# Expert outputs added into DRAM accumulators by accumulating scatters, in place of a slot store and a final gather

## What is computed

```python
def routed_experts(xt, idx, gate, w_exp_gu, w_exp_down):
    ...
    def run_block(args):
        tok, g, e = args
        return swiglu(x_pad[tok], w_exp_gu[e], w_exp_down[e]) * g[:, None]
    out = lax.map(run_block, (row_tok.reshape(n_blocks, MOE_BLOCK), ...))
    return jnp.zeros((T + 1, D), xt.dtype).at[row_tok].add(out.reshape(R, D))[:T]

def layer(x, pos, past, p):
    ...
    x = layer_norm(ALPHA * x + moe(x, w_router, ...), ln2_g, ln2_b)   # moe = routed + shared
```

## Time and profile before

| | |
|---|---|
| median of three runs | 2325.43 us (2324.3 to 2326.22) |
| span of the profiled execution, first to last instruction | 2317.7 us |
| PE busy | 2065.0 us, 89% of the span |
| DVE busy | 1156.8 us, 50% |
| POOL busy | 529.5 us, 23% |
| moved by DMA | 408.86 MB |

### The profile page before, as it was taken

How to read it: one execution, slowest core, us unless ns; L and a number is a source line. 1 busy time by engine, 2 the same in 40 slices (tenths; PEclk the granted TensorE clock), 3 DMA queues, 4 the chain that set the end, 5 groups by cost and what they waited for, 6 DMA issues and landing times.

```text
span 2317.7 us, 24124 instructions
## 1 busy us (share of the span) xinstructions
PE 2065.0 (89%) x8178; PEld 1163.1 (50%) x8178; DVE 1156.8 (50%) x2206; ACT 505.6 (22%) x1011; POOL 529.5 (23%) x888
## 2 busy tenths in 40 slices
PE   8998699999998999998999999999999999999300
PEld 6754275655564655565454554445544444444100
DVE  5205599999996679760355631111111111111487
ACT  2324441000124650030132001111111111111100
POOL 0088840000120001101222330000000001110487
PEclk9999799999998999999999999999999999999755
DMA  4160005443210012014311208999999999999765
GB/s 125 45 66 3 1 4 191 163 143 125 96 35 5 1 28 55 27 53 152 120 55 37 109 21 315 368 368 367 367 370 368 366 369 365 373 364 365 273 236 165
DMA packets 144789, 408.86 MB, mean 176 GB/s; under 512 B 31490, under 2 KB 79619, under 8 KB 126915
## 3 DMA queue, kind: packets, MB, share of 16 engines
q1 hardware_dynamic: 103602, 281.30, 35.5%
q0 software_dynamic: 17328, 62.92, 7.3%
q10 hardware_dynamic: 23776, 63.57, 7.0%
HBM read 333.10 MB, written 74.40 MB: 176 GB/s over the span
## 4 chain that ended last, share of the span: by engine, by line
PE 59%; DVE 22%; POOL 9%; issue 6%; ACT 2%; DMA 1%; SPq 0%; POOLq 0%; DVEq 0%; ACTq 0%
PE psum L816 20%; PE psum L830 10%; DVE arena L1648 9%; DVE best L1647 8%; PE psum L682 7%; PE psum L700 5%; PE psum L808 3%; PE psum L753 2%; POOL arena L1205 2%; PE psum L617 2%; ACT arena L1218 2%; PE psum L636 2%; POOL sct L1094 2%; PE psum L603 2%; PE psum L744 1%
## 5 line engine op out<-in xcount | busy, mean ns | idle before, releaser
L1218 ACT ACTIVATE arena<-psum 128x256 f32<-128x256 f32 (+8 forms) x714 | 334.5, 500 | 1506.2 <-PE psum L816 442.9
L816 PE MATMUL psum<-arena 128*128 128x512 f32 x1088 | 478.4, 593 | 1.1 <-DVE arena L1925 1.1
L816 PEld LDWEIGHTS psum<-arena 128*128 128x128 f32 x1088 | 202.2, 191 | 228.9 <-issue 227.9
L1930 DVE TENSOR_TENSOR arena<-arena,psum 128x256 f32<-128x256 f32 x68 | 28.7, 421 | 452.6 <-ACT arena L1218 452.6
L544 PE MATMUL psum<-arena 128*128 128x384 f32 (+1 forms) x768 | 239.1, 473 | 13.6 <-DVE arena L1673 8.4
L1647 DVE MAX8 best<-arena 128x8 f32<-128x384 f32 (+6 forms) x224 | 246.6, 1101 | 6.1
L830 PE MATMUL psum<-arena 128*128 128x512 f32 x544 | 244.8, 593 | 0.5 <-ACT arena L1218 0.5
L1648 DVE MATCH_REPLACE8 arena<-best,arena 128x384 f32<-128x384 f32 (+6 forms) x224 | 242.8, 1084 | 0.0
L544 PEld LDWEIGHTS psum<-arena 128*128 128x128 f32 x768 | 145.8, 191 | 106.5 <-DVE arena L1673 15.9
L682 PE MATMUL psum<-arena 128*128 128x384 f32 (+1 forms) x576 | 178.6, 473 | 5.9 <-DMA arena<-in_w_attn_proj 5.9
L1180 POOL TENSOR_TENSOR carry<-ones 1x1 f32<-1x1 f32 x67 | 12.2, 183 | 678.9 <-DVE tid L1889 678.9
(11 more groups left out here) (245 smaller groups left out, 2411.5 us busy)
## 6 DMA issues: line engine op xcount, KB each, us to landing
arena<-in_w_exp_gu SPq DMA_DIRECT2D x69, 2048.0 KB, 10.0
arena<-in_w_exp_down SPq DMA_DIRECT2D x68, 1024.0 KB, 10.5
slots_d<-arena ACTq DMA_DIRECT2D x68, 512.0 KB, 9.5
slots_d<-arena ACTq DMA_DIRECT2D x6, 3584.0 KB, 11.2
arena<-in_w_in SPq DMA_DIRECT2D x24, 512.0 KB, 4.4
slots_d<-arena ACTq DMA_DIRECT2D x2, 2816.0 KB, 9.2
arena<-in_x_prompt SPq DMA_DIRECT2D x10, 512.0 KB, 4.1
arena<-in_w_glu SPq DMA_DIRECT2D x16, 256.0 KB, 4.7
```

The lines of the kernel that those rows point to most:

```text
L816: last = mm(psum[:, 2, :], xgT[u][:, k, :], ewg[u][:, k, :], start=k == 0, stop=k == DK - 1)
L1218: return act.activation(dst, src, fn, **kw)
```

## The change

Instead of a slot per row, there are two DRAM accumulators `acc_d[0]` and `acc_d[1]`, each with one row per token and 128 rows more for padding. In the loop POOL, not ACT, issues the store of block n: an indirect DMA that adds the 128 rows of `yb[u]` to the rows of their tokens in `acc_d[u]` (`scatter`). No token stands twice in a block, and two scatters to one accumulator are kept apart by the wait for `y_stored{u}`. Padding rows have token numbers of their own behind the last token, so that each of the 128 destinations is different; `x1_d` has zero rows there.

`acc_d[0]` begins as `ALPHA*x + shared`: SP stores the nine tiles of `x1` there after the first expert loads, and POOL waits for those stores before its first gather. `acc_d[1]` and the padding rows are cleared early (6 transfers, about 6 MB, in place of the 8). After the loop SP loads each tile of both accumulators, DVE adds the two, and the end stage is written anew: small tiles are doubled, DVE's steps for three tiles are interleaved, and the multiplication by the LN2 weight moves from POOL to DVE. Two scatters to padding rows stand in the program ahead of routing, to set the first count of `y_stored`.

```diff
-        x1_d = dram("x1_d", (T, DM))
-        slots_d = dram("slots_d", (NBP * P, DM))
+        x1_d = dram("x1_d", (ACC, DM))
+        acc_d = [dram(f"acc{u}_d", (ACC, DM)) for u in range(2)]
...
+            for i in range(NT):
+                sp.wait_ge(s("base_ready"), i + 1)
+                ld(acc_d[0][tok(i), :], x1[0:rows(i), i, :], "base_stored")
             sp.wait_ge(s("egu_full"), 1)
             load_gu(expert(2), 0)
...
-            sp.nop().then_inc(s("slots_done"), 1)
+            for i in range(NT):
+                for u in range(2):
+                    ld((x1 if u == 0 else add1)[0:rows(i), i, :], acc_d[u][tok(i), :], f"acc_loaded{i}")
...
             pool.wait_ge(s("x1_stored"), 16 * NT)
+            pool.wait_ge(s("base_stored"), 16 * NT)
+
+            def scatter(u, rows_):
+                pool.indirect_dma_start(acc_d[u], bass.IndirectOffsetOnAxis(ap=sid[u][:, 0:1], axis=0), rows_, None,
+                                        compute_op=ALU.add).then_inc(s(f"y_stored{u}"), 16)
...
-                    pool.wait_ge(s("carried"), n + 1)
+                    pool.wait_ge(s("carried"), n * 2 + 1)
                     pool.wait_ge(s("tid_ready"), n + 4)
                     carry_wait()
                     gather(1 - u)
+                    pool.wait_ge(s("carried"), n * 2 + 2)
+                    pool.wait_ge(s("sid_ready"), n + 1)
+                    pool.wait_ge(s("y_half"), n * 2 + 2)
+                    carry_wait()
+                    scatter(u, yb[u])
...
-            for i in range(NT + 1):
-                for k in range(MK if i < NT else 0):
...
-                    pool.indirect_dma_start(part[0:rows(i), m % 8, :], None, slots_d,
...
-                    step(tt(y, y, ln2[0:r, 0, :], ALU.mult))
-                    tt(y, y, ln2[0:r, 1, :], ALU.add).then_inc(s("out_ready"), 1)
+            for i in range(NT):
+                y = x1[0:rows(i), i, :]
+                pool.wait_ge(s("scaled"), i + 1)
+                tt(y, y, ln2[0:rows(i), 1, :], ALU.add).then_inc(s("out_ready"), 1)
...
-            def store_y(u, n):
-                act.wait_ge(s("y_half"), (n + 1) * 2)
-                act.dma_start(slots_d[bass.ds(n * P, P), :], yb[u]).then_inc(s(f"y_stored{u}"), 16)
...
                 dve.wait_ge(s(f"y_stored{u}"), stores)
+                ts(sid[u][:], tab[:, 0, bass.ds(n, 1)], 1.0, None, ALU.mult).then_inc(s("sid_ready"), 1)
...
-                for k in range(MK):
-                    m = i * MK + k
-                    dve.wait_ge(s(f"part_loaded{m % 8}"), 16 * (m // 8 + 1))
-                    tt(x, x, part[0:r, m % 8, :], ALU.add).then_inc(s("part_used"), 1)
-                    dve.wait_ge(s("part_used"), m + 1)
-                statistics(x, r, NT + i)
+            def gather_up(i):
+                r, x = rows(i), x1[0:rows(i), i, :]
+                dve.wait_ge(s(f"acc_loaded{i}"), 32)
+                tt(x, x, add1[0:r, i, :], ALU.add).then_inc(s("summed"), 1)
+                dve.wait_ge(s("summed"), i + 1)
+                variance(x, r, NT + i)
...
+            for i in range(NT + 2):
+                if i < NT:
+                    gather_up(i)
+                if 0 <= i - 1 < NT:
+                    scale_shift(rows(i - 1), NT + i - 1)
+                if 0 <= i - 2 < NT:
+                    scale_by_weight(i - 2)
```

More of the change, by code:

```diff
@@ L258, in layer_program @@
         tid = [sb(f"tid{u}", [P, 1], I32) for u in range(2)]
+        sid = [sb(f"sid{u}", [P, 1], I32) for u in range(2)]
+        dump = sb("dump", [P, 1])
         bexp = sb("bexp", [P, 4])
@@ L1080, in _ @@
             pool.memset(hp[:, 0, :, :], 0.0).then_inc(s("constants"), 1)
+            pool.iota(dump[:], [[0, 1]], base=T + 1, channel_multiplier=1,
+                      allow_small_or_imprecise_dtypes=True).then_inc(s("constants"), 1)
             pool.iota(bexp[:, 0:1], [[0, 1]], base=0, channel_multiplier=1,
@@ L1157, in _ @@
                 tt(x, x, ln1[0:r, 1, :], ALU.add).then_inc(s("x1_ready"), 1)
+            pool.wait_ge(s("acc_cleared"), 16 * 6)
+            pool.wait_ge(s("dump_ready"), 2)
+            for u in range(2):
+                pool.indirect_dma_start(acc_d[u], bass.IndirectOffsetOnAxis(ap=sid[u][:, 0:1], axis=0), ln1[:, u, :],
+                                        None, compute_op=ALU.add).then_inc(s(f"y_stored{u}"), 16)
             pool.wait_ge(s("slots_ready"), 1)
@@ L1330, in _ @@
                     act.wait_ge(s("zeros_ready"), 1)
[L1331 to L1334, removed]
+                    for j in range(2):
+                        half = slice(j * 512, j * 512 + 512)
+                        act.dma_start(acc_d[1][:, half].rearrange("(b p) f -> p b f", p=DEC),
+                                      zeros[0:DEC].unsqueeze(1).broadcast_to([DEC, ACC // DEC, 512])
+                                      ).then_inc(s("acc_cleared"), 16)
+                        act.dma_start(acc_d[0][T:ACC, half], zeros).then_inc(s("acc_cleared"), 16)
+                        act.dma_start(x1_d[T:ACC, half], zeros).then_inc(s("acc_cleared"), 16)
             def take_qkv(i):
@@ L1481, in _, with final_std, final_norm @@
             take_eh(1, last_pair * 2 + 2)
-            store_y(0, last_pair * 2)
             half_y(1, last_pair * 2 + 2)
-            store_y(1, last_pair * 2 + 1)
-            for i in range(NT):
-                r = rows(i)
+            def final_std(i):
                 act.wait_ge(s("var_ready"), NT + i + 1)
-                f(lst[0:r, 1:2], lst[0:r, 0:1], ACT.Sqrt).then_inc(s("std_ready"), 1)
+                f(lst[0:rows(i), (NT + i) % 2, 1:2], lst[0:rows(i), (NT + i) % 2, 0:1], ACT.Sqrt
+                  ).then_inc(s("std_ready"), 1)
+            def final_norm(i):
+                r, v = rows(i), (NT + i) % 2
                 act.wait_ge(s("rstd_ready"), NT + i + 1)
-                f(x1[0:r, i, :], x1[0:r, i, :], ACT.Identity, bias=lst[0:r, 3:4],
-                  scale=lst[0:r, 2:3]).then_inc(s("normed"), 1)
+                f(x1[0:r, i, :], x1[0:r, i, :], ACT.Identity, bias=lst[0:r, v, 3:4],
+                  scale=lst[0:r, v, 2:3]).then_inc(s("normed"), 1)
+            for i in range(NT + 1):
+                if i < NT:
+                    final_std(i)
+                if i > 0:
+                    final_norm(i - 1)
         @block.vector
@@ L1511, in _ @@
                             ldt[64:80, :].unsqueeze(2).broadcast_to([GP, 2, NS])).then_inc(s("param_rows"), 1)
+            dve.wait_ge(s("constants"), 9)
+            for u in range(2):
+                ts(sid[u][:], dump[:], -1.0, None, ALU.add).then_inc(s("dump_ready"), 1)
             ar, ai = par[:, 0, :], par[:, 1, :]
@@ L1787, in residual @@
                 dve.wait_ge(s("res_ready"), i + 1)
-                statistics(x, r, i)
+                variance(x, r, i)
+                scale_shift(r, i)
             def expert_match(i):
@@ L1899, in _ @@
                     dve.wait_ge(s("tab_ready"), 1)
+                    step(ts(empty, tab[:, 0, :], 0.0, dump[:, 0:1], ALU.is_equal, ALU.mult))
+                    step(stt(tab[:, 0, :], tab[:, 0, :], -1.0, empty, ALU.add, ALU.add))
                     list_rows(0, tab[:, 0, 0:1])
```

76 lines of the change are left out of this document (37 added, 39 removed).

## The result

| | before | after |
|---|---|---|
| median | 2324.86 us (4 runs, 2321.33 to 2326.22) | 2244.68 us (4 runs, 2240.84 to 2248.36) |
| ratio | | 0.9669, 95% interval 0.965 to 0.9688 |
| span of the profiled execution | 2317.7 us | 2246.5 us, of a run of 2248.36 us |
| moved by DMA | 408.86 MB | 374.64 MB |

The account below looks back on a forecast made before the run. PE was taken to set the loop's pace, DMA engines nearly full. 2317.7 + 10.7 (loop's start) + 8 (loop) - 84 (end stage) + 7.7 (median over span) = 2260 us; own bounds 2247 to 2297, range 2240 to 2446.

Parts of the forecast that it names:

- the one held likeliest: Whole kernel: PE sets the loop's pace, the end stage shortens, the loop starts later; 2247 to 2297 us, chance 0.54.
- Its signs: Blocks 11.4 to 11.6 us apart, first L808 8 us later, acc_d loads 7 us after last L1938, DVE turns 5 us.
- The end stage: After the last L1938: 54 gathers and 54 additions go, two loads and one addition per tile come; 84 us gained.
- the 0.5 allowed for collisions: End stage: 0.5 us of DVE's 5.0 us per tile, allowed for gaps and for collisions with POOL.
- The loop's start: Before the first L808: POOL waits for the base stores, the gather follows, PE's clock drops; 10.7 us lost (7.7 to 16.7).
- The loop: Each block's scatter adds 2.56 us of DMA work; 11.54 us per block, 0.12 over PE, 8 us in 66 blocks.
- the upper bound of 12.39: Loop, DMA time per block in us: SP's queue as before 8.55, gather 1.28, scatter 2.56; PE takes 11.42.
- the lower bound of 11.14: Loop, DMA time per block in us with SP's 3.15 MB at 431 GB/s, taking 7.30, plus gather and scatter.
- What lies around the span: Outside the profiled span: the runs' median 2325.43 us was 7.7 us above the span's 2317.7, added at the end.
- no room in the DMA engines: Loop: memory limits the rate, so a block takes 12.39 or 12.9 us; total 2316 or 2350 us; chance 0.17.
- accumulated rows hold their engine: Loop: engines wait for each destination's read; 0.49 us per row breaks even, 0.72 makes 2446 us in total; chance 0.22.
- The gather comes late: Loop: scatter and gather on POOL's queue land one after the other, 2.4 us late for PE; total 2410; chance 0.07.

Follow-up runs that it names:

- The late wait: The changed kernel with POOL's wait for the base stores moved behind its first three gathers: 2233.06 us, ratio 0.9629; a repeat 2232.65 us, 0.9641.
- all three runs in which DMA became the bound: The changed kernel with a second adding scatter per block, 2386.41 us; with the old store left in, 2305.6; with one eighth of L818 left out, 2218.56.

## Why the prediction was right

The forecast was 2260 us, and 2244.68 came. The mechanism was the one held likeliest: PE keeps the loop's pace, the end stage loses its gathers and additions, and the loop's start pays for a wait. Its signs came too: blocks 11.42 us apart, loads of the accumulators 6.6 us after the last L1968, and PE waiting for nothing from 1500 to 2000 us. But the time lies 2.3 us below the 2247 that the prediction gave as the lower end of that case; only the margin down to 2240 took it in. By its steps:

- *The end stage*: 84 us forecast, 88 measured. The last scatter's wait and the loads were sized right (DVE starts 11.3 us after the last L1968, forecast 11.1), a turn takes 4.49 us in place of 5.0: the 0.5 allowed for collisions was not needed. Beside POOL's one pass, DVE's additions and multiplications take 1.21 us in the median; it is POOL's pass that is long there, 3.25 us in the median, against 2.33 in the earlier trace rows.
- *The loop's start*: 10.7 us forecast, 11.4 measured. The step to the first L810 grew by 8.6 us against 8.2; the clock's part was 2.8 against 2.5, in the first L810 and L818. The late wait took both away. Not all of such a clock loss needs the wait, though: one execution with the late wait lost 1.5 us there too.
- *The loop*: +8 us forecast, none measured beside the clock's 2.8. This is the term that was mis-sized. The scatter's price was right to a tenth (2.80 us against 2.56; 0.35 us per row against 0.32, and 2.2 times a gather's). What was wrong was the weight given to SP's queue at its old 8.55 us, which made the upper bound of 12.39. It has no fixed need: it took 7.57 us with the scatter, 8.63 without the add, and 7.41 when PE asked for blocks faster, near the 7.30 worked out from the 431 GB/s. The demand per block, where a kernel with less work for PE shows it, is 11.07, next to the lower bound of 11.14, and PE's 11.42 stayed above it.
- *What lies around the span*: 7.7 us were added, and only 1.9 are there (2248.36 against 2246.5). It was a wrong reading: the 7.7 compared the span of one execution with the median of others. Other executions of the kernel before have 2.1 us around their span (2323.16 against 2321.1), by which the profiled one lay some 5 us below the median of its runs, while that of after lay 3.7 above. Against the span the forecast was 2252.4 us and 2246.5 came: 8 less in the loop, 4 less at the end, 0.7 more at the start and 5.3 more ahead of it, which is chance between executions. Medians against spans make up the other 9.5 us.

Of the rivals, *no room in the DMA engines* asked for 12.39 or 12.9 us per block and is ruled out by 11.42 and 11.07; *accumulated rows hold their engine* needed 0.49 us per row and found 0.35. *The gather comes late* didn't happen in the changed kernel, where it lands after 8.1 us, but it named the right place: in all three runs in which DMA became the bound, PE waited there and nowhere else (1500 to 2000 us). The one-after-the-other landing that it rested on is not what a block shows; a gather and a scatter land after 8.1 and 8.2 us within 11.42.

Still open: what makes the 11.07 us. One reading is the engines' throughput, the other the turn of the gather through POOL's queue: 14.0 us to land and about 8.1 us through PE, DVE and POOL until the next issue make two blocks of 11.07. For throughput speaks that in the changed kernel the same turn has some 6.6 us to spare (8.1 and 8.1 in two blocks of 11.42), so that the landing had to get that much longer first; and that one more store, on a queue of its own, costs 1.33 us per block over 11.07 and one more adding scatter 2.55, near their engine times of 1.28 and 2.65. No run separates the two, such as plain scatters with less work for PE.

## What to carry to other kernels

A busy share of 97% on the DMA engines didn't mean that they were full: the queue that holds most bytes gives way, and its need is read where its transfers stand behind one another, not from its share. When work is moved into a stage that two resources nearly fill, cut or add a known amount of one of them and see the spacing of the blocks: that gives the margin (0.35 us here), which the kernel's own busy shares didn't show. And put a new wait behind everything that doesn't need it: one line ahead of three gathers cost 6.5 to 9.3 us by the runs, and nine early loads in one queue cost more than they saved.

## What was not expected of the hardware

The DMA share of a stretch goes above 1 with adding scatters (1.02 in the loop, 1.03 with more of them), and the GB/s don't count the destinations that are read: 347 GB/s with two adding scatters per block, 397 with none, both at a share of 1.00 or more. An adding scatter holds POOL for 1.60 us at its issue, a plain one for 0.99 and a gather for 1.00. Alone, after the loop, the adding scatter lands after 6.1 us and a plain one after 3.3; under the loop's load the adding one takes 8.2, no longer than a plain one (8.1).
